# Top-2 expert rows weighted at eviction, fetched into four buffers and added by GpSimd

## What is computed

```python
def moe_ffn(h, w_router, w_gu, w_down):
    ht = h.reshape(B * S, D)                                   # 256 x 1024
    logits = (ht @ w_router).astype(jnp.float32)               # 8 experts
    top_vals, top_idx = lax.top_k(logits, TOP_K)               # TOP_K = 2
    top_w = jax.nn.softmax(top_vals, axis=-1)
    combine = jnp.sum(jax.nn.one_hot(top_idx, N_EXPERTS) * top_w[..., None], axis=1)
    out = jnp.zeros((B * S, D), jnp.float32)
    for e in range(N_EXPERTS):
        y = swiglu(ht, w_gu[e], w_down[e], D_FF_EXPERT)        # D_FF_EXPERT = 1792
        out = out + combine[:, e:e + 1] * y.astype(jnp.float32)
    return out
...
x = x + moe_ffn(h, moe_router[i // 2], moe_w_gu[i // 2], moe_w_down[i // 2])
```

## Time and profile before

| | us |
|---|---|
| median of 3 runs | 1243.52 (1242.11 to 1243.96) |
| the profiled execution | 1242.05 |
| its span in the trace | 1240.3 |
| routing of layer 1 | about 704 to 721 |
| experts 0 to 7 of layer 1 | about 721.6 to 1204 |
| rest (scatter, gate, last norm) | 1204 to 1240 |

### The profile page before, as it was taken

The page is one execution under the profiler, slowest core; times in us unless marked ns, Lnnn a source line. Parts: engine busy times, 40 slices in busy tenths (PEclk is TensorE's granted clock), DMA queues, the critical chain, the costliest instruction groups (busy, mean ns, idle before and its releaser), DMA issues.

```text
span 1240.3 us, 15364 instructions
## 1 busy us (share of the span) xinstructions
PE 1211.2 (98%) x5976; PEld 1008.3 (81%) x5976; DVE 901.6 (73%) x864; ACT 721.5 (58%) x677; POOL 112.7 (9%) x131
## 2 busy tenths in 40 slices
PE   8999999999999999999999999999999999999997
PEld 6887787788888887897778878888888888888876
DVE  6767755654444467657766578898898988888996
ACT  5446544534343456335643467878777777777765
POOL 4700000200000010340000000001000001000301
PEclk9999999999999999999999899999999999999999
DMA  9945454656565555555445489999999999999970
GB/s 294 320 145 195 136 177 162 230 178 200 174 202 175 199 161 186 165 201 170 136 165 174 153 274 376 364 388 375 388 378 387 388 382 385 384 387 379 392 281 35
DMA packets 152204, 317.55 MB, mean 256 GB/s; under 512 B 6273, under 2 KB 41345, under 8 KB 152146
## 3 DMA queue, kind: packets, MB, share of 16 engines
q1 hardware_dynamic: 147328, 302.27, 69.6%
q0 software_dynamic: 4112, 13.44, 3.0%
q10 hardware_dynamic: 706, 1.07, 0.3%
HBM read 310.99 MB, written 5.77 MB: 255 GB/s over the span
## 4 chain that ended last, share of the span: by engine, by line
PE 82%; DVE 9%; ACT 5%; issue 3%; DMA 1%; SPq 0%; POOL 0%; POOLq 0%; ACTq 0%; DVEq 0%
PE ps L1783 22%; PE ps L1528 15%; PE ps L1529 14%; PE ps L1530 14%; PE ps L1770 11%; DVE split L961 3%; ACT split L615 3%; DMA raw<-w_in_dram 1%; PE ps L1750 1%; PE ps L1618 1%; DVE M L1336 1%; DVE hT L993 1%; PE ps L1544 1%; PE ps L1644 1%; PE ps L1739 1%
## 5 line engine op out<-in xcount | busy, mean ns | idle before, releaser
L961 DVE TENSOR_TENSOR split<-raw,split 128x2048 fp32r<-128x2048 f32 x281 | 644.6, 2298 | 242.2 <-ACT split L615 240.0
L615 ACT ACTIVATE split<-raw 128x2048 fp32r<-128x2048 f32 x281 | 538.2, 1916 | 264.2 <-PE ps L1530 190.4
L1783 PE MATMUL ps<-split,br 128*128 128x512 f32 x1344 | 317.5, 392 | 1.5 <-DVE br L1083 1.0
L1783 PEld LDWEIGHTS ps<-split,br 128*128 128x128 f32 x1344 | 249.4, 188 | 56.1 <-issue 2.0
L1528 PE MATMUL ps<-split,hT 128*128 128x512 f32 (+1 forms) x608 | 240.0, 395 | 8.4 <-DVE hT L993 3.3
L1529 PE MATMUL ps<-split,hT 128*128 128x512 f32 (+1 forms) x608 | 234.6, 386 | 0.0
L1530 PE MATMUL ps<-split,hT 128*128 128x512 f32 (+1 forms) x608 | 234.6, 386 | 0.0
L1770 PE MATMUL ps<-split,hT 128*128 128x512 f32 x672 | 159.7, 392 | 0.1
L1770 PEld LDWEIGHTS ps<-split,hT 128*128 128x128 f32 x672 | 124.8, 188 | 28.0 <-issue 1.6
L1528 PEld LDWEIGHTS ps<-split,hT 128*128 128x128 f32 x608 | 115.3, 190 | 36.1 <-DVE hT L993 5.7
L1530 PEld LDWEIGHTS ps<-split,hT 128*128 128x128 f32 x608 | 115.3, 190 | 23.1
(11 more groups left out here) (248 smaller groups left out, 934.7 us busy)
## 6 DMA issues: line engine op xcount, KB each, us to landing
raw<-moe_w_gu_dram SPq DMA_DIRECT2D x96, 1024.0 KB
raw<-moe_w_down_dram SPq DMA_DIRECT2D x56, 1024.0 KB
raw<-w_in_dram SPq DMA_DIRECT2D x45, 1024.0 KB
raw<-ffn_w_gu_dram SPq DMA_DIRECT2D x28, 1024.0 KB
raw<-moe_w_gu_dram SPq DMA_DIRECT2D x32, 512.0 KB
raw<-ffn_w_down_dram SPq DMA_DIRECT2D x14, 1024.0 KB
raw<-w_branch_dram SPq DMA_DIRECT2D x12, 1024.0 KB
raw<-w_out_dram SPq DMA_DIRECT2D x8, 1024.0 KB
```

What stands on the lines that cost most here:

```text
L615: act.activation(split[:, t % SPLIT, 0, :], raw[:, t % RAW, :], ACT.Copy).then_inc(hi, 1)
L961: dve.tensor_tensor(split[:, t % SPLIT, 1, :], raw[:, t % RAW, :], split[:, t % SPLIT, 0, :].bitcast(F32), ALU.subtract).then_inc(lo, 1)
L1783: ins = pe.matmul(ps[:, 5 if kind == "up" else 4, :], xe[:, sl, 4 * part + k, :], slot(t, sr, 512)[:, k, :], start=part + k + m == 0, stop ...
```

## The change

Five edits that belong together:

1. The slots' weights are made in the routing. ACT's `weight_exp` moves from expert 0 to just behind `store_y(1)`, DVE's `token_weights` from expert 1 to just ahead of the two tile splits that close the routing, with four more instructions that write `w_hot` (the one-hot of each pick times its weight). PE multiplies the slot lists with it (`slot_weights`, four f32 matmuls behind `proj_part(1, 1)`), and DVE copies the result to `slot_w`.
2. ACT's evictions of experts 0 to 6 (L750) take `slot_w` as their per-row scale, so the rows are stored with their weight.
3. `ye_rows1` has one more row of zeros, written by a DMA from POOL at the program's start. A pick that belongs to expert 7 or to the second pass reads that row (`ZERO_ROW`), so no weight is needed in the add.
4. `picks(1)` fetches into four buffers (`Y[:, 0]`, `Y[:, 1]`, and the old `qT` and `kT`) with no wait between the four fetches.
5. POOL itself adds them to X (`tensor_tensor`, 128x1024), one after another; DVE's four `add_pick` in expert 7 go. `add_last` waits for POOL's adds.

```diff
+        pick_rows = [Y[:, 0, :], Y[:, 1, :], spare[0], spare[1]]
...
             pool.wait_ge(consts, 9)
+            pool.dma_start(ye_rows[1][ZERO_ROW:ZERO_ROW + 1, :], kT[0:1, :, :, :].rearrange("p h s n -> p (h s n)")
+                           ).then_inc(zero_row, 16)
...
             def picks(s):
 
+                if s == 1:
+                    pool.wait_ge(picked, 1)
+                    for n in range(2 * NB):
+                        pool.indirect_dma_start(pick_rows[n], None, ye_rows[1][:, :], bass.IndirectOffsetOnAxis(
+                            pick_row[:, 0, n // 2, n % 2:n % 2 + 1], 0)).then_inc(picks_in[n], 16)
+                    for n in range(2 * NB):
+                        b = n // 2
+                        pool.wait_ge(picks_in[n], 16)
+                        if n % 2:
+                            pool.wait_ge(picks_used, n)
+                        pool.tensor_tensor(X[:, b, :], X[:, b, :], pick_rows[n], ALU.add).then_inc(picks_used, 1)
+                    return
...
-                    if s == 1 and i == 0 and j == 1:
-                        weight_exp()
...
-                        act.activation(rows_out[:, cols(nh)], ps[:, nh, :], ACT.Copy).then_inc(down_free[s], 1)
+                        if s == 1 and i + nh == 0:
+                            act.wait_ge(w_ready, 2)
+                        act.activation(rows_out[:, cols(nh)], ps[:, nh, :], ACT.Copy,
+                                       scale=slot_w[:, i:i + 1] if s == 1 else 1.0).then_inc(down_free[s], 1)
...
                     store_y(1)
+                    weight_exp()
                     proj_out_of(1, 0)
                     experts(1, t0 + T_FFN[1])
...
-                    if s == 1 and i == 1 and j == AT_WEIGHTS[0]:
-                        token_weights()
...
-                    if last and s == 1 and j in AT_COMBINE:
-                        add_pick(1, AT_COMBINE.index(j))
...
+                for b in range(NB):
+                    for k in range(2):
+                        ins = dve.tensor_scalar(w_hot[:, b, k, :], hot[:, b, k, :], wts[:, b, 2 + k:3 + k], None,
+                                                ALU.mult)
+                ins.then_inc(w_ready, 1)
+
+            def slot_weights():
+
+                dve.wait_ge(route_done[1], 2)
+                dve.tensor_copy(slot_w[:, :], ps[:, 7, SEQ + EXPERTS:SEQ + 2 * EXPERTS]).then_inc(w_ready, 1)
...
+                if nh == 0:
+                    dve.wait_ge(picks_used, 2 * (b + 1))
                 dve.wait_ge(scattered, 2 * nh + b + 1)
...
                     dve.tensor_copy(more_i[:, :], most[:, 1:2]).then_inc(routed, 1)
+                    token_weights()
                     split_lo(t0 + T_OUT + 5)
                     split_lo(t0 + T_OUT + 6)
+                    slot_weights()
                     experts(1, t0 + T_FFN[1])
...
+            def slot_weights():
+
+                pe.wait_ge(w_ready, 1)
+                for b in range(NB):
+                    for k in range(2):
+                        ins = pe.matmul(ps[:, 7, SEQ + EXPERTS:SEQ + 2 * EXPERTS], prT[:, 2 * b + k, :],
+                                        w_hot[:, b, k, :], start=b + k == 0, stop=b + k == NB)
+                ins.then_inc(route_done[1], 1)
...
                     proj_part(1, 1)
+                    slot_weights()
                     pe.wait_ge(proj_out, NB + 1)
                     more = experts(1, t0 + T_FFN[1])
```

More of the change, by code:

```diff
@@ L96 @@
 AT_LAST = 18
-AT_COMBINE = (8, 9, 13, 14)
+ZERO_ROW = (EXPERTS - 1) * P
 AT_WEIGHTS = (6, 9, 12)
@@ L197, in trunk @@
         slot_tok = sb("slot_tok", [P, EXPERTS], U32)
+        slot_w = sb("slot_w", [P, EXPERTS])
+        w_hot = sb("w_hot", [P, NB, 2, EXPERTS])
         nth = sb("nth", [P, NB, 2, EXPERTS])
@@ L290, in trunk @@
         rows_free = [None] + [sem(f"rows_free{i}") for i in (1, 2)]
+        w_ready, zero_row = sem("w_ready"), sem("zero_row")
         picked, picks_used = sem("picked"), sem("picks_used")
-        picks_in = [sem(f"picks_in{i}") for i in range(2)]
+        picks_in = [sem(f"picks_in{i}") for i in range(4)]
         gT_turned, gT_ready = sem("gT_turned"), sem("gT_ready")
@@ L647, in mean_square, with weight_exp @@
                                accum_out=ms[:, b, nh:nh + 1]).then_inc(ms_ready, 1)
+            def weight_exp():
+                act.wait_ge(sel_ready, 3)
+                for b in range(NB):
+                    ins = act.activation(wts[:, b, 1:2], wts[:, b, 0:1], ACT.Exp, scale=rstd[:, b:b + 1])
+                ins.then_inc(route_step, 1)
             def store_y(b):
@@ L701, in gather_hi @@
                                ).then_inc(xe_hi[s], 1)
-            def weight_exp():
-                act.wait_ge(sel_ready, 3)
-                for b in range(NB):
-                    ins = act.activation(wts[:, b, 1:2], wts[:, b, 0:1], ACT.Exp, scale=rstd[:, b:b + 1])
-                ins.then_inc(route_step, 1)
             def expert(s, t0, i, last):
@@ L1118, in add_pick @@
                                          op0=ALU.mult, op1=ALU.add).then_inc(picks_used, 1)
-                dve.wait_ge(picks_used, 4 * (s - 1) + n + 1)
+                dve.wait_ge(picks_used, 2 * NB + n + 1)
             def expert(s, t0, i, last):
@@ L1196, in token_picks @@
                         chain(dve.tensor_scalar(row, row, -float(P), None, ALU.add))
-                    chain(dve.tensor_tensor(pick[:, 5], row, mine, ALU.mult))
+                        chain(dve.tensor_tensor(pick[:, 5], row, mine, ALU.mult))
+                    else:
+                        chain(dve.scalar_tensor_tensor(out=pick[:, 5], in0=row, scalar=-float(ZERO_ROW), in1=mine,
+                                                       op0=ALU.add, op1=ALU.mult))
+                        chain(dve.tensor_scalar(pick[:, 5], pick[:, 5], float(ZERO_ROW), None, ALU.add))
                     chain(dve.tensor_copy(pick_row[:, i], pick[:, 5]))
@@ L1218, in experts @@
                 if s == 2:
+                    dve.wait_ge(picks_used, 2 * NB)
                     for n in range(2 * NB):
@@ L1347, in _ @@
                         dve.wait_ge(qk_turned, 3 * l + 3)
+                        dve.wait_ge(zero_row, 16)
                         for s in range(2):
```

6 lines of the change are left out of this document (3 added, 3 removed).

## The result

The median of seven executions each rose from 1243.52 (1242.11 to 1244.47) to **1247.43 us** (1245.94 to 1248.07); the ratio is 1.0034, with a 95% interval of 1.0024 to 1.0043. The profiled execution took 1246.28 us with a span of 1244.5, where that of before took 1242.05 with 1240.3. The page first: busy times, as the earlier trace rows for the kernel before.

The account below looks back on a forecast made before the run. PE was taken to set the pace, with DVE closest behind. Terms -1.0 + 5.5 + 1.0 - 0.9 = +4.6 us on the median of 1243.52 gave 1248.1; range 1246.4 to 1251.6, low end extended to 1244.5.

Parts of the forecast that it names:

- Part 1: Expert 7: four adds of 1.28 us leave DVE, where most of their time was hidden; -1.0 us.
- Part 2: Expert 7: POOL's adds delay DVE's splits and make PE wait; +5.5 us, between +4.2 and +8.6.
- Part 3: Expert 7: four fetches at once, 2 MB in 11 us, make ACT wait for no DMA; 0.
- Part 4: Routing: four f32 matmuls on PE's path cost +1.0 us, between 0.85 and 1.04; DVE's added instructions cost 0.
- Part 5: Expert 0: ACT's table load and exponents leave, shortening PE's wait for the first SwiGLU product; -0.9 us (0 to -1.2).
- case (C): Expert 7: POOL's adds run between DVE's splits and each holds the next one; chance 0.82.
- The hold: Expert 7: POOL's add waits for one DVE split, then holds the next for 2.3 us.
- the floor without a stall: Expert 7 without a stall would take 59.25 us, worked from 60.03 us an expert.
- The lead: Expert 7: splits are ready 1.2 us before PE needs them, taken once off a loss of 6.7 us.
- When the adds begin: Expert 7: four fetch issues of some 2.9 us each, then POOL's adds from about 1163 to 1181.4.
- Rival (A): Expert 7: POOL's adds fall into DVE's gaps or hold it only partly; -0.9, 1242.6 us; chance 0.14.
- Rival (B): Expert 7: the clock falls with PE idle 1.7 of every 4.5 us; +9, 1257 us; chance 0.04.

Follow-up runs that it names:

- no_adds: Changed kernel with POOL's four adds left out, fetches and waits kept: 1242.06 us, ratio 0.9985 to the kernel before.
- E7: A clock read from timelines, not a run: time between the first evictions of experts 6 and 7; 60.27 us before the change, 64.61 after.
- E0: A clock read from timelines, not a run: time from expert 0's first matmul to its first eviction; 60.93 us before the change, 59.98 after.
- alone: Kernel before with only ACT's table load and two exponents moved from expert 0 to the routing: 1241.87 us, ratio 0.9989.
- one input: Changed kernel with each of POOL's adds replaced by a multiplication by 1.0 from the fetch buffer into X: 1243.02 us.
- memsets: Changed kernel with each of POOL's adds replaced by two memsets of 128x1024, which only write SBUF: 1240.2 us.
- adds_twice: Changed kernel with each of POOL's adds run twice, the first into the fetch buffer: 1253.34 us, ratio 1.0078 to the kernel before.
- quarters: Changed kernel with each of POOL's adds cut into four of 128x256, eleven executions: 1241.18 us, ratio 0.9984 to the kernel before.

## Why the prediction was right, step by step

The profiled execution took 1246.28 - 1242.05 = 4.23 us longer. The terms, each with what the runs gave it:

| step | predicted | measured | from |
|---|---|---|---|
| Part 1, adds leave DVE | -1.0 | -1.62 | before against `no_adds`, E7 |
| Part 2, adds on POOL | +5.5 | +5.96 | after against `no_adds`, E7 |
| Part 3, fetches | 0 | none seen | `no_adds` has them |
| Part 4, routing | +1.0 | +0.73 | timeline; PE's step for it 0.81 |
| Part 5, exponents | -0.9 | -0.95 | E0; alone -0.89 |
| sum | +4.6 | +4.12 | profile +4.23, medians +3.9 |

Two stages outside the terms nearly cancel: the changed kernel reached the conversion of `more_i` 0.31 us later (713.72 against 713.41; in the other kernels 713.3 to 715.9), and expert 1 gained 0.27. The prediction had put the latter at 0, because PE does not wait there.

The forecast of 1248.1 stands 0.7 us above the median of 1247.43. Its mechanism is case (C), and the things it named are all there: splits up to 4.5 us, four waits of PE of about 1.2 us, E7 at 64.61 (63.5 to 65), a clock at 1.00. The details by their steps:

- **The hold.** The one pair of rows of layer 0's pooling gave the rule, from an add of 256 columns: it waits for one split and holds the next for its whole length. It held for one four times as long. The own time of 2.2 (1.88 to 2.97) was right too: each of the four adds ends 2.26 or 2.27 us behind the split that it waited for, and holds of 2.09, 2.19, 1.60 and 2.21 us follow, the 1.60 where a SwiGLU product of DVE ran beside the add. No 1024-column add ran with DVE idle. The Trainium skill (GPSIMD Engine Reference, Elementwise — side-by-side cycle accounting) gave an estimate of 2.25, and these rows agree with it. Against one sentence of it the measurement decides: the skill (SBUF — State Buffer, Who interferes with whom) has a two-input DVE instruction and a GpSimd one that reads exclude each other for the whole instruction; for two inputs 2.2 us were held of the 2.26 that the add ran behind the split ahead of it, which agrees, but for one input 0.83 of 2.65 us. That only a reading instruction of GpSimd interferes, as the same section says, `memsets` shows: 0.
- **Part 1 was mis-sized**, -1.0 where -1.62 was there. The step that failed is the floor without a stall: I worked it out as 59.25 from the mean of six experts, and `no_adds` reaches 58.65. The 0.6 us are no work of PE. The mean of 60.03 holds expert 1 with its 60.66; experts 2 to 6 take 59.90. And the clock by evictions starts late: expert 6's stands behind a split of ACT (1141.04 + 1.92 us in `no_adds`) and starts 4.95 us after PE's last stretch of matmuls in that expert began (1137.92), expert 7's comes without such a split, 4.40 after the same point (1197.12). 59.90 - 1.04 + 0.26 - 0.55 = 58.57. The same error hides in Part 2: from the true floor the adds cost 5.96, and the two errors, +0.6 and -0.5, nearly cancel in the difference, which was predicted at +4.5 and came to +4.34.
- **The lead** was put at 1.2 us; `adds_twice` puts it at 0.84. That is 0.36 of the 0.46 by which Part 2 was too small. The excess at a tile was right by luck: DVE's cycle was put at 4.54 us and was 4.41, PE's pace at 2.86, a mean with transposes, and was 2.72, so 1.68 was forecast and 1.69 measured. 4 x 1.69 - 0.8 = 5.96.
- **The range.** Its upper end takes -0.5 for Part 5, whose own range ends at 0; with 0 it would be 1252.1 and not 1251.6. Nothing hangs on it here.
- **When the adds begin.** I had the fourth fetch issue for 2.9 us like the others, and the adds from 1163. It took 0.94, and they began at 1160.95. It changed nothing, since the expert had room on both sides. The last issue starts where DVE runs no split (1159.91, between 1159.38 and 1160.25); each of the three ahead of it starts beside a split and ends 0.81 to 0.84 us behind it. The other traces agree: in `no_adds` and `memsets` the first issue too finds no split, or the last tenth of a microsecond of one, and takes 0.97. By these rows a fetch's issue waits out a split as an add does; no run varied it.
- **Part 4.** PE's matmuls took 0.96 (0.85 to 1.04), of which 0.81 lie ahead of the next matmul (719.83 to 720.64). The routing as a whole grew by 0.73 only: the embedding's product ahead was 0.11 shorter, as the clock rose 2.1 us behind the conversion and not 2.5, and the transposes behind took 0.03 more. Over all traces the routing takes 8.97 to 9.52 us with the slots' weights (ten traces) and 8.24 to 8.61 without (four); the means differ by 0.9. The forecast of 1.0 stands, and the 0.73 is a little lucky. DVE's 2 to 2.5 us and the zero row cost nothing, as their covers said. The evictions with a scale take 0.67 where they took 0.57; up to expert 6 none of it reached the path.
- **Part 5.** The wait of PE was expected at 0.3 and fell to 0.55, while the expert gained what was forecast, 0.95.

**Rival (A)**, that the hold does not bite, is what quarters come near to: (A) forecast -0.9, and with them the median is 1241.18 against 1242.96 for the kernel before, executed beside it, with E7 1.1 us shorter. The prediction named the point from which it decides (0.3 us an add, for four); for many pieces the rows put it near 0.5 us at one tile, PE's 2.72 less the split's 2.24. **Rival (B)** did not occur with PE busy 3.09 of 5 us, nor in `adds_twice`.

## What to carry to other kernels

Work that is moved from a nearly full engine to an idle one is free only as long as the two do not take turns at something: look in the trace for any place where both already run on SBUF, and take the price from the stretching of the instruction that was there first, not from the busy time of the idle engine. Where such turns are unavoidable, cut the moved work so that one turn fits into what the paced engine has free in one cycle of the bounding engine (here about 0.5 us of 2.72); four times the instructions with a quarter of the columns cost 0.5 us instead of 6. And measure the floor of a stage with the disputed work taken out before an attribution: 0.6 of the 1.6 us that the old adds cost had been hidden, in a mean and in where the stage's clock started.
